# The down projection of a decoder block: weight sums moved from GpSimd to VectorE, rounds of six pairs instead of four, and a plain, row-tiled end

## The reference

```python
D_MODEL = 2048; SEQ = 512; D_FF = 4 * D_MODEL; EPS = 1e-6

def rms_norm(x, g):
    xf = x.astype(jnp.float32)
    y = xf * lax.rsqrt(jnp.mean(xf * xf, axis=-1, keepdims=True) + EPS)
    return (y * g.astype(jnp.float32)).astype(x.dtype)

# ... x = x + rms_norm(mixed, norm_mix_post[l])
h2 = rms_norm(x, norm_mlp_pre[l])
a = jax.nn.relu(h2 @ w_up[l])                       # (512, 8192)
x = x + rms_norm((a * a) @ w_down[l], norm_mlp_post[l])
```

## Time and profile before

| what | value |
|---|---|
| median of 3 runs | 2479.56 us (2478.64 to 2480.72) |
| the profiled execution: its own time, its span | 2481.26 us, 2479.6 us |
| PE busy | 2412.3 us, 97%, 11482 matmuls |
| DVE, ACT, POOL busy | 1553.5, 812.7, 953.2 us |
| mean granted TensorE clock | 0.991 |
| HBM traffic over the span | 173 GB/s |

### The profile page before, as it was taken

The page is one execution under the profiler, slowest core; times in us unless marked ns, Lnnn a source line. Parts: engine busy times, 40 slices in busy tenths (PEclk is TensorE's granted clock), DMA queues, the critical chain, the costliest instruction groups (busy, mean ns, idle before and its releaser), DMA issues.

```text
span 2479.6 us, 30028 instructions
## 1 busy us (share of the span) xinstructions
PE 2412.3 (97%) x11482; PEld 1956.1 (79%) x11482; DVE 1553.5 (63%) x1775; ACT 812.7 (33%) x1073; POOL 953.2 (38%) x771
## 2 busy tenths in 40 slices
PE   9999999999999999999999999999999999999984
PEld 7866887877888888898888888888777878778763
DVE  8875688896434432364444444444478788787887
ACT  5145223333422222252222222222233333333332
POOL 1120334440000000002222222222399999999985
PEclk9999999999999999999999999999999999999997
DMA  6431333443434453344565455555476777667733
GB/s 222 113 115 52 114 121 107 132 124 102 127 95 151 142 182 101 103 169 174 191 249 219 169 189 182 191 187 174 168 254 230 265 282 252 230 228 282 273 126 148
DMA packets 98557, 430.04 MB, mean 173 GB/s; under 512 B 19552, under 2 KB 19616, under 8 KB 88448
## 3 DMA queue, kind: packets, MB, share of 16 engines
q1 hardware_dynamic: 65392, 266.89, 32.3%
q0 software_dynamic: 10432, 80.12, 9.2%
q10 hardware_dynamic: 22608, 81.31, 8.9%
HBM read 350.62 MB, written 77.66 MB: 173 GB/s over the span
## 4 chain that ended last, share of the span: by engine, by line
PE 75%; POOL 10%; DVE 10%; ACT 2%; issue 2%; DMA 1%; ACTq 0%; DVEq 0%; POOLq 0%
PE main L1840 20%; PE main L1842 20%; PE main L1841 20%; DVE wd_lo L1716 5%; DVE mlp_acc L1727 3%; POOL wd_sums L576 3%; POOL wd_sum_third L579 2%; POOL wd_sums L572 2%; POOL wd_sums L577 2%; POOL wd_sums L573 1%; ACT wd_hi L990 1%; PE side L2058 1%; PE side L2060 1%; PE side L2059 1%; PE main L2058 1%
## 5 line engine op out<-in xcount | busy, mean ns | idle before, releaser
L1840 PE MATMUL main<-h_hi,w_hi 128*128 128x512 f32 x1792 | 704.3, 393 | 2.2 <-DVE h_lo L1085 2.1
L1842 PE MATMUL main<-h_hi,w_lo 128*128 128x512 f32 x1792 | 697.9, 389 | 0.0
L1841 PE MATMUL main<-h_lo,w_hi 128*128 128x512 f32 x1792 | 697.6, 389 | 0.0
L1069 DVE TENSOR_TENSOR w_lo<-w_raw,w_hi 128x1024 fp32r<-128x1024 f32 x307 | 383.4, 1261 | 299.6 <-ACT w_hi L621 293.1
L621 ACT ACTIVATE w_hi<-w_raw 128x1024 fp32r<-128x1024 f32 x307 | 317.5, 1053 | 422.7 <-PE main L1842 320.4
L1840 PEld LDWEIGHTS main<-h_hi,w_hi 128*128 128x128 f32 x1792 | 336.4, 188 | 77.3 <-issue 4.8
L1842 PEld LDWEIGHTS main<-h_hi,w_lo 128*128 128x128 f32 x1792 | 336.3, 188 | 70.7
L1841 PEld LDWEIGHTS main<-h_lo,w_hi 128*128 128x128 f32 x1792 | 336.5, 188 | 67.9
L1716 DVE TENSOR_TENSOR wd_lo<-wd_sums,wd_hi 128x1024 fp32r<-128x1024 f32 x128 | 210.4, 1644 | 105.5 <-ACT wd_hi L994 65.6
L555 POOL TENSOR_TENSOR a_blocks<-a_blocks 128x512 f32<-128x512 f32 x32 | 42.2, 1319 | 400.1 <-DVE a_blocks L1669 400.1
L1668 DVE TENSOR_TENSOR a_blocks<-main,rstd_mlp 128x1024 f32<-128x1024 f32 x32 | 39.2, 1224 | 213.7 <-PE main L1842 205.1
(11 more groups left out here) (362 smaller groups left out, 4427.2 us busy)
## 6 DMA issues: line engine op xcount, KB each, us to landing
w_raw<-wstream SPq DMA_DIRECT2D x307, 512.0 KB, 3.6
wd_raw<-wdown SPq DMA_DIRECT2D x128, 768.0 KB, 5.3
...
a_second_group<-a_scratch ACTq DMA_DIRECT2D x32, 768.0 KB, 7.2
...
```

Of the source, the lines that this page charges most:

```text
L1069: tt(WL[:, s], RAW[:, s], WH[:, s].bitcast(F32), ALU.subtract).then_inc(lo_ready, 1)
L1840: mm(o, wh, xh[:, k0 + k], start=first and k == 0, stop=False)
L1841: mm(o, wh, xl[:, k0 + k], start=False, stop=False)
L1842: ins = mm(o, wl, xh[:, k0 + k], start=False, stop=last and k == 3)
```

## The change

1. **Double weight sums on DVE.** `weight_sums` on POOL is gone. DVE makes two of the sums of a set with one instruction of 128x1024 (`two_sums`, L1785 of the new kernel), one operand of which is one block read twice. For that the scheme of products is another variant, in which both sums share a block. POOL keeps one sum of 128x512 per second set (`third_sum`, L632).
2. **Rounds of six pairs.** Five rounds of six pairs, 120 sets; products add up over six sets before they are gathered. Two more buffers each for the first and second group; the two that lie where the up stage has its staging tiles are loaded by SP (L433, L434) once all pairs are stored. In the first round ACT, not DVE, copies the finished products out of PSUM (`first_copy`).
3. **Plain last two pairs.** Pairs 30 and 31 are multiplied with eight plain products and need no sums of activations or weights. On cb 0 they go set by set into four pairs of banks, on cb 1 row tile by row tile, both pairs at once, so that a row tile of the last columns is finished while PE works on the next.
4. **The end by tile.** POOL combines all seven groups for both column blocks (`combine`, L645). DVE adds the plain products of each row tile, ACT takes its squares and root, and DVE scales it and adds the residual rows while PE is busy with the next; the last tile is done in halves.

```diff
-N_ROUND, N_SET = 8, 128
+N_ROUND, PER, N_SET = 5, 6, 120
...
-        FIRST = ((0, 2, S21), (1, 1, S5), (2, 0, S12), (3, 3, S22))
-        SECOND = ((0, 0, S11), (1, 2, S4), (2, 1, S7))
+        FIRST = ((0, 3, S21), (1, 2, S5), (2, 1, S22), (3, 0, S12))
+        SECOND = ((0, 2, S4), (1, 1, S7), (2, 0, S11))
...
+        def set_part(s, half):
+            if s >= N_SET:
+                return PLAIN[s - N_SET][:, 2 * half:2 * half + 2]
+            if half == (1 if is_first(s) else 0):
+                return TS[s % 2][:]
+            return RAWD[s % 3][:, 1:3] if is_first(s) else T3[third_of(s) % 2][:].unsqueeze(1)
...
+                if s == 0:
+                    sp.wait_ge(lo_ready, N_UNIT - 4)
+                elif s < 3:
+                    sp.wait_ge(lo_ready, N_UNIT - 3 + s)
                 else:
-                    sp.wait_ge(wd_sum, sums_until(s - 3))
+                    sp.wait_ge(wd_sum, s - 2)
                     if is_first(s - 3):
                         sp.wait_ge(wd_lo, 2 * s - 5)
-                sp.dma_start(RAWD[:, s % 3], wdown[s // 8, s % 4][:, weights_of(s)]).then_inc(wd_landed[s % 3], 16)
+                    else:
+                        sp.wait_ge(wd_third, third_of(s - 3) + 1)
+                if s == PER:
+                    sp.wait_ge(a_stored, 16 * N_PAIR)
+                    sp.wait_ge(unit_done, N_UNIT)
+                    for kk in (4, 5):
+                        sp.dma_start(AF[kk][:], a_dram[kk][:, 0:4]).then_inc(ax_landed[kk], 16)
+                        sp.dma_start(AS[kk][:], a_dram[kk][:, 4:7]).then_inc(ay_landed[kk], 16)
+                sp.dma_start(RAWD[s % 3][:], wdown[s // (2 * PER) % 2, s // (4 * PER) * PER + s % PER][:, weights_of(s)]
+                             ).then_inc(wd_landed[s % 3], 16)
+            sp.wait_ge(prod_done, N_PROD - 3)
+            for s in range(4):
+                sp.dma_start(PLAIN[s][:], wdown[s // 2, N_PAIR - 2 + s % 2]).then_inc(plain_landed[s], 16)
+            sp.wait_ge(prod_done, N_PROD)
+            sp.dma_start(G3[:], gain_rows[1:2].to_broadcast([P, D])).then_inc(g3_landed, 16)
+            for t in range(TT_N):
+                sp.dma_start(X1F[t][:], x1_dram[t]).then_inc(x1_back, 16)
...
+            def third_sum(s):
+                n = third_of(s)
                 pool.wait_ge(wd_landed[s % 3], 16 * (s // 3 + 1))
-                if s >= 2:
-                    pool.wait_ge(wd_lo, 2 * s - 2)
-                if is_first(s):
-                    b12, b11, b22 = raw
-                    ptt(TS[:, t0], b12, b22, ALU.subtract)
-                    ptt(TS[:, t0 + 1], b11, b12, ALU.add).then_inc(wd_sum, 1)
-                else:
-                    b11, b22, b21 = raw
-                    ptt(TS[:, t0], b11, b22, ALU.add)
-                    ptt(TS[:, t0 + 1], b21, b11, ALU.subtract).then_inc(wd_sum, 1)
-                    pool.wait_ge(wd_lo, 2 * s)
-                    ptt(TS2[:], b21, b22, ALU.add).then_inc(wd_sum, 1)
+                if n >= 2:
+                    last = (n - 2) // PER * 2 * PER + PER + (n - 2) % PER
+                    pool.wait_ge(wd_lo, 2 * last + 2)
+                ptt(T3[n % 2][:], RAWD[s % 3][:, 0], RAWD[s % 3][:, 1], ALU.subtract).then_inc(wd_third, 1)
...
+                pool.wait_ge(prod_read, 7 * (2 * N_ROUND - 2 + cb) + (4 if i < 3 else 7))
...
+            for s in range(N_SET):
+                if not is_first(s):
+                    third_sum(s)
+                for cb in range(2):
+                    first = N_SET - 3 * PER + 2 * PER * cb
+                    if first + 2 <= s < first + 5:
+                        combine(cb, s - first - 2)
+                    if s == first + 5:
+                        for i in range(3, 8):
+                            combine(cb, i)
+            for i in range(4):
+                by_gain(i)
...
+            def first_copy(s, j):
...
+                act.wait_ge(prod_done, k + 1)
+                nc.scalar.activation(ACC[:, s // (2 * PER), products_of(s)[j][2]], prod_banks(k), ACT.Copy
+                                     ).then_inc(prod_read, 1)
...
+            for s in range(N_SET + 2):
+                n = len(products_of(s)) if s < 4 * PER and s % PER == PER - 1 else 0
+                for half, js in enumerate((range(0, min(2, n)), range(2, n))):
+                    for j in js:
+                        first_copy(s, j)
+                    down_hi(s + 2, half)
...
+            def two_sums(s):
+                o, raw, pair_ = pair_sums(s)
+                one = raw[:, 0:1] if is_first(s) else raw[:, 2:3]
+                v.wait_ge(wd_landed[s % 3], 16 * (s // 3 + 1))
+                if s >= 2:
+                    v.wait_ge(wd_lo, 2 * s - 2)
+                elif s == 1:
+                    v.wait_ge(lo_ready, N_UNIT)
+                tt(o[:], one.to_broadcast([P, 2, T]), pair_, ALU.add).then_inc(wd_sum, 1)
...
+                v.wait_ge(prod_read, k)
+                tt(o, prod_banks(k), o, ALU.add).then_inc(prod_read, 1)
...
+                if s + 3 < N_SET:
+                    two_sums(s + 3)
                 n = len(products_of(s))
                 for half, js in enumerate((range(0, 2), range(2, n))):
-                    for j in js if s % 4 == 3 else ():
-                        if last and not is_first(s):
-                            last_second(s // 8 % 2, j)
-                        else:
-                            if last and j == 3:
-                                v.wait_ge(early_ready, 3 * (s // 8 % 2) + 1)
-                            gather(s, j)
-                    if s + 2 < N_SET:
-                        down_lo(s + 2, half)
-                if last and s % 8 == 3:
-                    last_first(s // 8 % 2)
...
+                    for j in js if s % PER == PER - 1 and s >= 4 * PER else ():
+                        gather(s, j)
+                    down_lo(s + 2, half)
...
+            def rows_out(t, cb, r=slice(0, 2)):
+                x = (first_rows, scaled_rows)[cb](t)[:, r]
+                y = X1F[t][:, cb * 1024 + r.start * T:cb * 1024 + r.stop * T].rearrange("p (n c) -> p n c", c=T)
+                stt(out=x, in0=x, scalar=ROW[:, 7, t:t + 1], in1=y, op0=ALU.mult, op1=ALU.add).then_inc(out_ready, 1)
...
+            def half_sum(m):
+                t = TT_N - 1
+                v.wait_ge(tail_done, t + m + 1)
+                link_to(tt(last_rows(t)[:, m], plain_banks(t)[:, m], last_rows(t)[:, m], ALU.add), row_sum, t + m + 1)
+                tt(scaled_rows(t)[:, m], last_rows(t)[:, m], G3L[:, m], ALU.mult)
+            v.wait_ge(block_ready, 16)
+            for t in range(TT_N - 1):
+                v.wait_ge(tail_done, t + 1)
+                link_to(tt(last_rows(t), plain_banks(t), last_rows(t), ALU.add), row_sum, t + 1)
+                if t == 0:
+                    v.wait_ge(g3_landed, 16)
+                tt(scaled_rows(t), last_rows(t), G3L, ALU.mult)
+                if t < TT_N - 2:
+                    v.wait_ge(x1_back, 16 * TT_N)
+                    row_inverse(t)
+                    v.wait_ge(scaled, 4)
+                    rows_out(t, 0)
+                    rows_out(t, 1)
+            half_sum(0)
+            row_inverse(TT_N - 2)
+            rows_out(TT_N - 2, 0)
+            t = TT_N - 1
+            v.wait_ge(fsq_ready, 2 * TT_N + t + 1)
+            stt(out=ROW[:, 4, t:t + 1], in0=ROW[:, 5, t:t + 1], scalar=1.0 / D, in1=ROW[:, 4, t:t + 1],
+                op0=ALU.mult, op1=ALU.add).then_inc(fb_ready, 1)
+            half_sum(1)
+            rows_out(TT_N - 2, 1)
+            row_inverse(t)
+            for cb in range(2):
+                for c in range(2):
+                    rows_out(t, cb, slice(c, c + 1))
...
+            WHOLE = ((1, 0), (3, 2))
+            def plain(s, kh, i, q, o, first, last):
+                w, b = WHOLE[kh][i % 2], set_buffer(s)
+                return down_mm(o, AF[s % 2].bitcast(F32R), 2 * kh + i // 2, slice(q * P, q * P + P),
+                               WHD[b][:, w], WLD[b][:, w], first, last)
+            s = N_SET
+            pe.wait_ge(ax_landed[0], 16 * (N_ROUND + 1))
+            for kh in range(2):
+                pe.wait_ge(wd_lo, 2 * s + kh + 1)
+                for i in range(4):
+                    if kh == 0:
+                        pe.wait_ge(prod_read, N_PROD + i - 3)
+                    for q in range(2):
+                        ins = plain(s, kh, i, q, prod_banks(N_PROD + i)[:, q], kh == 0, False)
+                ins.then_inc(wd_done, 1)
+            pe.wait_ge(ax_landed[1], 16 * (N_ROUND + 1))
+            pe.wait_ge(wd_lo, 2 * s + 4)
+            for i in range(4):
+                for q in range(2):
+                    for kh in range(2):
+                        ins = plain(s + 1, kh, i, q, prod_banks(N_PROD + i)[:, q], False, kh == 1)
+                ins.then_inc(prod_done, 1)
+            pe.wait_ge(wd_lo, 2 * s + 8)
+            for t in range(TT_N):
+                for n in range(2):
```

(8 more changed lines are left out.)

392 lines of the change are left out of this document (179 added, 213 removed).

## The result

| | us |
|---|---|
| kernel before, median of 4 runs | 2479.85 |
| changed kernel, median of 4 runs (lowest, highest) | 2444.32 (2442.78, 2445.30) |
| ratio, 95% interval | 0.9857 [0.9839, 0.9874] |
| profiled execution: its time, its span | 2442.78, 2441.1 |
| predicted | 2414, range 2404 to 2436 |

The change brings 36 us where 65 were forecast. The direction was right; the time lies outside the range.

The account below looks back on a forecast made before the run. It took PE as losing 66 us in the down stage, waiting on DVE and, through ACT, POOL's sums, plus 21.3 us after. Unbroken end 2397.7 + 3 + 3 + 2 + 8.6 = 2414.3 us, range 2404 to 2436.

Parts of the forecast that it names:

- start of the stage: Down stage's first sets: PE loses 3 us, for set 6's weights landing at 1807 to 1809; bounds 0 and 11.6.
- group ends and transfers: Down-stage loop: 0.3 us lost in each of ten column blocks, 3 us (bounds 0 and 14); loads cost nothing.
- plain sets and the end: Last window: plain sets need no sums, POOL's last five combinations end in time; 2 us lost, bounds 0 and 15.
- behind the last matmul: Work left after PE's last matmul, from a half's addition to the last store: 8.6 us, bounds 7.5 and 21.3.
- 2397.7: Down stage's end if 2712 matmuls run at the unbroken pace, 615.0 us from 1782.7.
- all 8.1 us of POOL's third sums: Per six pairs in the loop, POOL's remaining sums could all delay DVE, then at 54.0 of 57.2 us.
- The transfers' bound of 6 us: Loop loads on cb 1, six second sets in a row at 385 GB/s: taken as nothing, at most 6 us.
- late at the product changes or in the transfers: Rival, chance 0.22: thin margins at group ends or late loads cost 14 or 6 us, giving 2425.
- the pace: PE in the down stage without waits: one matmul start every 0.2268 us.
- the 5.4 us of more PE work: Down stage: 2712 matmuls, 24 more than before, add 5.4 us.
- DVE not setting the pace: Against the rival, chance 0.05, that DVE's list in every set makes the kernel slower, 2480 to about 2507.
- ACT's copies: First round's product copies on ACT: priced at 1.06 us each, four fitting between its hi parts in 5.44 us.

Follow-up runs that it names:

- x1: The changed kernel with POOL's 16 combinations cut to 8 of 512 columns each, so the output is incomplete; 2422.8 us.
- x4: The changed kernel with DVE's gathers and lo parts ahead of the double sum in each group's last set, same computation; 2431.6 us.
- x6: The changed kernel with activation reloads from the second round on cut to one block of the four or three; 2436.5 us.

## Why the prediction was wrong

| term | predicted | measured |
|---|---|---|
| start of the stage | 3 | 0.8 (block 1) |
| group ends and transfers | 3 + 0 | 13.4: 11.3 in blocks 4 to 8, 2.1 in blocks 9 and 10 of x1 |
| plain sets and the end | 2 | 19.7 (33.9 less the two above) |
| behind the last matmul | 8.6 | 9.5 |

With 2397.7 that is the span of 2441.1.

**The step that failed is the term of the plain sets and the end, 2 us with a bound of 15.** It priced POOL's combinations only for when POOL would be done with them. I even had the length: five in 14 to 23 us was the estimate, 16.6 is measured. What they take from DVE was left out of the sum, although the same text set all 8.1 us of POOL's third sums against DVE. Eleven of the sixteen stand in two blocks; at 2.2 us each that is 24 us of DVE. By the prediction's own numbers a block has 57.2 - 54.0 = 3.2 us of room with the third sums counted, so 24.2 - 6.4 = 18 us would have been the term; 19.7 is measured. That this comes so near is in part luck: of the 19.7 some 5.5 are the slow clock behind the waits, which the sum leaves out, and block by block it is less good (3.4 us for three combinations where block 9 has 6.2, 14.4 for eight where block 10 has 13.5). The five that the prediction did price, those beside the plain sets, cost nothing. The trace of before held the row. There POOL's L589, the same instruction, stands beside a lo part (POOL, then DVE):

```profile
2398.66 2.41 POOL L589 TENSOR_TENSOR mlp_acc<-mlp_acc 128x1024 f32<-128x1024 f32 x1
...
2404.55 2.39 POOL L589 TENSOR_TENSOR mlp_acc<-mlp_acc 128x1024 f32<-128x1024 f32 x1
```

```profile
2399.84 1.23 DVE L1754 TENSOR_TENSOR mlp_acc<-main,mlp_acc 128x1024 f32<-128x1024 f32 x1
...
2404.69 3.34 DVE L1716 TENSOR_TENSOR wd_lo<-wd_sums,wd_hi 128x1024 fp32r<-128x1024 f32 x1
```

Beside the first combination DVE reads PSUM and keeps its 1.23 us. Beside the second it reads two operands from SBUF and takes 3.34. I read means by line, in which six such instructions vanish among 128.

**The group ends were mis-sized**: 0.3 us for each of ten, measured 1.1 on cb 0 and 3.0 on cb 1. The place was right (DVE's double sum, gathers and lo parts in a group's last set, a margin of 0.8 us), and I took the low side of my bounds, because DVE had 11 us of room per block. Room on the mean says nothing of one set: x4 gets 9.9 of these 11.3 us back with the same instructions in another order. The transfers' bound of 6 us was what they cost (3 x 2.1 in x6), and I had taken 0. The rival "late at the product changes or in the transfers" came true in its size as well: x1, which has it without the combinations, is at 2422.8 for 2425 forecast. The combinations stand on top.

**Right were:** the pace and the 5.4 us of more PE work; the stage's start, with set 6's double sum beginning at 1807.11 after 5.55 us of waiting for weights (forecast 1807 to 1809) and PE losing less than a microsecond; DVE not setting the pace (x1 loses 13.9 us in the stage with every double sum on DVE); ACT's copies, 1.03 us against 1.06 priced; plain sets without loss; and the tail. Its last rows, for the earlier trace rows:

```profile
2432.00 0.69 DVE L1847 TENSOR_TENSOR mlp_acc<-side,mlp_acc 128x512 f32<-128x512 f32 x1
...
2434.72 2.74 DVE L1842 SCALAR_TENSOR_TENSOR mlp_acc<-mlp_acc,row_scalars,x_back 128x512 f32<-128x512 f32 x4
```

From the last matmul's end (2431.60) 0.4 us to the addition, 2.7 to the first output half, 2.7 for the four and 3.6 to the end of the span.

The rule of the Trainium skill that I weighed (SBUF — State Buffer, Who interferes with whom) was the one that decided the case. The trace bears it out with 3.24 to 3.42 us for 1.22, and with PSUM reads and fills that leave DVE alone. I applied it to the instructions that the change moved to DVE and not to those that it gave to POOL.
